# Up-projections of the third and fourth gated network as seven half-block products in place of eight

## What is computed

```python
def conv_ffn(a, w_up, conv_w, w_down):
    g, u = jnp.split(dwconv3(a @ w_up, conv_w), 2, axis=-1)
    return (jax.nn.silu(g) * u) @ w_down

h = h + g2 * conv_ffn(modulate(rms_norm_2(h, norm_ffn[i]), sh2, sc2), ffn_w_up[i], ffn_conv[i], ffn_w_down[i])
```

## Time and profile before

| what | value |
|---|---|
| median of 3 runs | 2995.22 us (2992.68 to 2999.0) |
| the profiled execution | 2993.15 us |
| its span, first to last instruction | 2991.4 us |
| PE busy | 2913.9 us, 97% |
| DVE, ACT, POOL busy | 60%, 43%, 16% |
| PE on the chain that ended last | 93% |

### The profile page before, as it was taken

How to read it: one execution, slowest core, us unless ns; L and a number is a source line. 1 busy time by engine, 2 the same in 40 slices (tenths; PEclk the granted TensorE clock), 3 DMA queues, 4 the chain that set the end, 5 groups by cost and what they waited for, 6 DMA issues and landing times.

```text
span 2991.4 us, 46812 instructions
## 1 busy us (share of the span) xinstructions
PE 2913.9 (97%) x19658; PEld 2583.3 (86%) x19658; DVE 1797.0 (60%) x2666; ACT 1300.3 (43%) x2153; POOL 483.1 (16%) x405
## 2 busy tenths in 40 slices
PE   6998999999999999999999999999999999999999
PEld 6997887899999999999999977667888878788887
DVE  7776664579597453547949757655535543465453
ACT  4575664344243455644424445654323332343231
POOL 0002221123032000002303313001202111121020
PEclk9998997999999999999999999999999999999999
DMA  2210000245554321025545520102232222223232
GB/s 103 89 53 36 2 2 6 75 156 183 170 170 164 113 88 36 1 79 183 176 164 189 188 99 29 43 17 83 94 97 88 97 90 93 91 85 101 90 97 86
DMA packets 79554, 284.34 MB, mean 95 GB/s; under 512 B 8528, under 2 KB 9296, under 8 KB 78576
## 3 DMA queue, kind: packets, MB, share of 16 engines
q1 hardware_dynamic: 79344, 281.35, 28.1%
HBM read 274.96 MB, written 6.36 MB: 94 GB/s over the span
## 4 chain that ended last, share of the span: by engine, by line
PE 93%; DVE 4%; ACT 2%; issue 1%; POOL 1%; DMA 0%; SPq 0%; DVEq 0%; ACTq 0%
PE psum L348 67%; PE psum L2733 2%; PE psum L1893 2%; PE psum L912 2%; PE psum L2104 2%; PE psum L2086 1%; PE psum L2077 1%; PE psum L1269 1%; PE psum L848 1%; PE psum L539 1%; PE psum L1319 1%; PE psum L1286 1%; PE psum L2430 1%; PE psum L2727 1%; PE psum L2721 1%
## 5 line engine op out<-in xcount | busy, mean ns | idle before, releaser
L303 DVE TENSOR_TENSOR wlo<-wraw,whi 128x1024 fp32r<-128x1024 f32 (+2 forms) x398 | 507.7, 1297 | 614.7 <-ACT whi L296 605.8
L296 ACT CAST whi<-wraw 128x1024 fp32r<-128x1024 f32 (+2 forms) x398 | 396.3, 1021 | 495.2 <-PE psum L348 460.6
L431 DVE CUSTOM_DVE_ANT_0 araw<-araw,cond 128x1024 f32<-128x1024 f32 x112 | 181.1, 1654 | 0.0
L348 PE MATMUL psum<-f0xh,whi 128*128 128x264 f32 x704 | 143.1, 285 | 0.0
L348 PE MATMUL psum<-f0xh,wlo 128*128 128x264 f32 x704 | 143.0, 285 | 0.0
L348 PE MATMUL psum<-f0xl,whi 128*128 128x264 f32 x704 | 142.4, 284 | 0.0
L348 PE MATMUL psum<-f1xh,whi 128*128 128x258 f32 x704 | 141.9, 283 | 0.0
L348 PE MATMUL psum<-f1xh,wlo 128*128 128x258 f32 x704 | 141.9, 283 | 0.0
L348 PE MATMUL psum<-f1xl,whi 128*128 128x258 f32 x704 | 141.4, 282 | 0.0
L348 PE MATMUL psum<-f2xh,whi 128*128 128x512 f32 x352 | 139.1, 395 | 1.0 <-DVE f2xl L592 1.0
L348 PE MATMUL psum<-f3xh,whi 128*128 128x512 f32 x352 | 139.1, 395 | 1.0 <-DVE f3xl L592 1.0
(11 more groups left out here) (515 smaller groups left out, 8193.9 us busy)
## 6 DMA issues: line engine op xcount, KB each, us to landing
wraw<-d_w SPq DMA_DIRECT2D x357, 512.0 KB, 3.4
araw<-d_ada SPq DMA_DIRECT2D x112, 512.0 KB, 3.3
wraw<-d_w SPq DMA_DIRECT2D x32, 384.0 KB, 3.6
hn<-d_h SPq DMA_DIRECT2D x4, 528.0 KB, 7.9
hres<-d_h SPq DMA_DIRECT2D x1, 2112.0 KB, 8.2
spill<-hres SPq DMA_DIRECT2D x1, 2112.0 KB, 7.4
hres<-spill SPq DMA_DIRECT2D x1, 2112.0 KB, 8.5
cond<-d_cond SPq DMA_DIRECT2D x2, 1024.0 KB, 4.8
```

The source lines that it names most:

```text
L296: e.copy(whi[0:rows, n % NH, 0:kt * cols], wraw[0:rows, n % NR, 0:kt * cols]).then_inc(*w_hi.up(n))
L303: e.tensor_tensor(wlo[0:rows, n % NH, 0:kt * cols], wraw[0:rows, n % NR, 0:kt * cols], whi[0:rows, n % NH, 0:kt * cols].bitcast(F32), ALU. ...
L348: ins = e.matmul(psum[0:bw, b0 + nb * len(sl) + si, 0:ln], l_ if z == 2 else h_, (xp.lo if z == 1 else xp.hi)[:, k, o:o + ln], start=k == ...
L431: e.tensor_tensor_reduce(out=w, in0=w, in1=self.c[:, col, :], scale=1.0, scalar=0.0, op0=ALU.mult, op1=ALU.add, accum_out=ada[:, ly, blk, ...
```

## The change

In f2 and f3 all pairs but the first two (`PLAIN = 2`) multiply by Strassen's scheme on one level. A pair is a product of a weight matrix of 256 columns by 1024 rows and 512 tokens; each of the three extents is halved, and the eight half-block products become seven of sums and differences of the halves.

- **TensorE**: seven products of 12 matmuls (4 blocks by hi/lo 3) over 256 tokens, 84 in place of 48 of 512 tokens. Products 0 and 1 start in banks b and b + 3. Product 2 adds on top of a copy of bank b in bank b + 1, products 4 and 6 in bank b + 2 on top of a copy of b + 1 (`quad_pe`).
- **ACT**: seven roundings of 128 by 512 in place of two of 128 by 1024; two copies from PSUM to PSUM, two from PSUM into `U` and one from PSUM into `p7`, all of 256 tokens, in place of two copies of 512; the first tap of gate and of value, which DVE had before.
- **DVE**: seven subtractions for `wlo` of 128 by 512 in place of two of 128 by 1024; four taps in place of six; two additions of 256 tokens from PSUM and `p7`.
- **POOL**: four sums of weights per pair, 128 by 512 each (`w_sum_pool`), beside the two operations on the hidden values that it had.
- **Once per network**: sums of the normalized tokens, POOL 16 operations of 128 by 256 and one small one, ACT and DVE twelve each for hi and lo (`turned`).
- `whi` and `wlo` now have six slots of 512 columns: an item is split when the item six half slots before it has been used. SP waits for the last reader of a raw chunk, for its first chunk also for POOL's last sum.

The diff, cut to its core:

```diff
--- before.py
+++ after.py
...
+SEVEN = ("f2", "f3")
+PLAIN = 2
+def by_seven(tag, j):
+    return isinstance(tag, tuple) and tag[0] in SEVEN and tag[1] == "up" and 11 * tag[2] + j >= PLAIN
...
+        for key in ([(n, i) for i in range(7)] if k == 0 else []) if seven else [(n,)]:
+            wide = 1 if seven else 2
+            pos += pos % wide
+            place[key] = pos % halves
+            users = [last[h % halves] for h in range(pos, pos + wide) if h % halves in last]
+            if users:
+                prev[key] = max(users)
+                freed.setdefault(prev[key], []).append(key)
+            for h in range(pos, pos + wide):
+                last[h % halves] = key
+            pos += wide
...
         def w_dma(e, n):
             _, _, _, kt, rows, cols = PLAN[n]
-            if n >= NR:
-                e.wait_ge(*w_lo.at(n - NR))
+            m = n - NR
+            if m >= 0:
+                tag, j, k, *_ = PLAN[m]
+                if not by_seven(tag, j):
+                    e.wait_ge(*w_lo.at(m))
+                elif k == 0:
+                    e.wait_ge(*w_lo.at(m, 4))
+                    e.wait_ge(*w_sum.at(m, 3))
+                else:
+                    e.wait_ge(*w_lo.at(m - 1, 6))
...
+        def factor_of(n, i):
+            return (quarter(n, 0), pair_sum(n), quarter(n, 1), quarter(n + 1, 0), quarter(n, 0), quarter(n + 1, 1),
+                    quarter(n + 1, 0))[i]
...
+        def w_sum_pool(e, n, s):
+            if s == 0:
+                g = SUMS.index((n, 0)) // 4
+                raw_here(e, n)
+                if g >= 2:
+                    e.wait_ge(*w_lo.at(SUMS[4 * g - 8][0], 1))
+                e.tensor_tensor(pair_sum(n), quarter(n, 0), quarter(n, 1), ALU.subtract).then_inc(*w_sum.up(n, 0))
+            elif s == 1:
+                raw_here(e, n + 1)
+                e.wait_ge(*w_sum.at(n, 0))
+                e.tensor_tensor(quarter(n, 1), quarter(n + 1, 1), pair_sum(n), ALU.subtract).then_inc(*w_sum.up(n, 1))
+            elif s == 2:
+                e.wait_ge(*w_sum.at(n, 1))
+                e.wait_ge(*w_lo.at(n, 0))
+                e.tensor_tensor(quarter(n, 0), quarter(n, 1), quarter(n, 0), ALU.add).then_inc(*w_sum.up(n, 2))
+            else:
+                e.wait_ge(*w_lo.at(n, 3))
+                e.tensor_tensor(quarter(n + 1, 0), quarter(n + 1, 0), quarter(n, 1), ALU.subtract).then_inc(*w_sum.up(n, 3))
+        def w_freed(e, split, *key):
+            for item in FREED.get(key, ()):
+                split(e, *item)
...
+            steps = [(b, X(0, first)), (b + 3, T(2)), (b + 1, T(3)), (b, X(4, first)), (b + 2, T(0)), (b + 1, T(1)),
+                     (b + 2, X(4, second))]
+            for i, (bank, operand) in enumerate(steps):
+                e.wait_ge(*w_lo.at(n, i))
+                if i == 0 and bank_free(f, p, 0):
+                    e.wait_ge(*bank_free(f, p, 0))
+                elif i == 1 and bank_free(f, p, 3):
+                    e.wait_ge(*bank_free(f, p, 3))
+                elif i == 2:
+                    e.wait_ge(*f_ev.at(f, p, 0))
+                elif i == 4:
+                    e.wait_ge(*f_ev.at(f, p, 1))
+                elif i == 6:
+                    e.wait_ge(*f_ad.at(f, p, 0))
+                wh, wl = w_place(whi, n, i), w_place(wlo, n, i)
+                for k in range(4):
+                    if p == PLAIN and i == 1:
+                        e.wait_ge(*f_tl.at(f, k, 3))
+                    for z in range(3):
+                        ins = e.matmul(psum[:, bank, 0:half], (wl if z == 2 else wh)[:, k, :], operand(z, k),
+                                       start=i < 2 and k == 0 and z == 0, stop=k == 3 and z == 2, skip_group_check=True)
+                ins.then_inc(*w_used.up(n, i))
...
+            def quad(p, behind):
+                n, b = quad_chunk(f, p), quad_bank(p)
+                if behind:
+                    second_out(p - 1)
+                w_freed(e, w_split_act, *AHEAD[(n, 0)])
+                if behind:
+                    tap(p - 1, 0)
+                e.wait_ge(*w_used.at(n, 0))
+                if bank_free(f, p, 1):
+                    e.wait_ge(*bank_free(f, p, 1))
+                e.activation(psum[:, b + 1, 0:half_], psum[:, b, 0:half_], ACT.Copy).then_inc(*f_ev.up(f, p, 0))
+                w_freed(e, w_split_act, n, 0)
+                e.wait_ge(*w_used.at(n, 1))
+                if p - 2 >= (PLAIN if p < 11 else 11):
+                    e.wait_ge(*f_ad.at(f, p - 2, 1))
+                e.activation(F.p7[:, p % 2, :], psum[:, b + 3, 0:half_], ACT.Copy).then_inc(*f_ev.up(f, p, 7))
+                w_freed(e, w_split_act, n, 1)
+                if behind:
+                    tap(p - 1, 1)
+                e.wait_ge(*w_used.at(n, 2))
+                if bank_free(f, p, 2):
+                    e.wait_ge(*bank_free(f, p, 2))
+                e.activation(psum[:, b + 2, 0:half_], psum[:, b + 1, 0:half_], ACT.Copy).then_inc(*f_ev.up(f, p, 1))
+                w_freed(e, w_split_act, n, 2)
+                e.wait_ge(*w_used.at(n, 3))
+                if p - 2 >= (0 if p < 11 else 11):
+                    e.wait_ge(*f_c.at(f, 2 * (p - 2), 2))
+                e.activation(up_slot(F, 2 * p, 0), psum[:, b, 0:half_], ACT.Copy).then_inc(*f_ev.up(f, p, 2))
+                w_freed(e, w_split_act, n, 3)
+                if behind:
+                    silu(p - 1)
+                w_freed(e, w_split_act, n, 4)
+                w_freed(e, w_split_act, n, 5)
+                if behind:
+                    hidden(p - 1)
...
+            def quad(p, behind):
+                n, b = quad_chunk(f, p), quad_bank(p)
+                w_freed(e, w_split_dve, *AHEAD[(n, 0)])
+                w_freed(e, w_split_dve, n, 0)
+                if behind:
+                    tap(p - 1, 0, 1)
+                w_freed(e, w_split_dve, n, 1)
+                if behind:
+                    tap(p - 1, 0, 2)
+                w_freed(e, w_split_dve, n, 2)
+                if behind:
+                    tap(p - 1, 1, 1)
+                w_freed(e, w_split_dve, n, 3)
+                if behind:
+                    tap(p - 1, 1, 2)
+                e.wait_ge(*f_ev.at(f, p, 7))
+                e.wait_ge(*w_used.at(n, 4))
+                e.tensor_tensor(up_slot(F, 2 * p + 1, 1), psum[:, b + 2, 0:half_], F.p7[:, p % 2, :],
+                                ALU.add).then_inc(*f_ad.up(f, p, 0))
+                w_freed(e, w_split_dve, n, 4)
+                e.wait_ge(*w_used.at(n, 5))
+                e.tensor_tensor(up_slot(F, 2 * p + 1, 0), psum[:, b + 1, 0:half_], F.p7[:, p % 2, :],
+                                ALU.add).then_inc(*f_ad.up(f, p, 1))
+                w_freed(e, w_split_dve, n, 5)
...
+            sums(0)
+            sums(1)
+            weights(PLAIN, (0,))
+            e.wait_ge(*n_lov.at(f, 7))
+            e.memset(F.U[:, :, 0:F.lead], 0.0).then_inc(*zeroed.up(f, 0))
+            e.memset(F.U[:, :, ntok + 1:ntok + 2], 0.0).then_inc(*zeroed.up(f, 1))
+            sums(2)
+            sums(3)
+            weights(PLAIN, (1, 2))
+            hidden(0)
+            weights(PLAIN, (3,))
+            rest(0)
+            for half in range(2):
+                for p in range(11 * half if half else PLAIN, 11 * half + 11):
+                    more_ = p % 11 < 10
+                    if more_:
+                        weights(p + 1, (0, 1, 2))
+                    if p > 11 * half:
+                        hidden(p - 1)
+                    if more_:
+                        weights(p + 1, (3,))
+                    if p > 11 * half:
+                        rest(p - 1)
+                hidden(11 * half + 10)
+                rest(11 * half + 10)
+                if not half:
+                    weights(11, range(4))
...
-            ffn_pe(e, F2, lambda e: e.wait_ge(*res.at("wino", 5)))
+            ffn7_pe(e, F2, lambda e: e.wait_ge(*res.at("wino", 5)))
```

310 lines of the change are left out of this document (269 added, 41 removed).

## The result

The changed kernel takes 3118.77 us (median of four runs, 3116.46 to 3122.09), the kernel before 2996.97 in the same comparison: a ratio of 1.0409 with the interval 1.0391 to 1.0427, 122 us more. The forecast was 3104, 109 more.

The account below looks back on a forecast made before the run. TensorE bounds the kernel before; after the change DVE, taking turns with POOL, bounds the up-projection pairs. Steady pairs 81, edge pairs 1 and starts 27 give +109 us, 3104 us with the median's offset; range 3070 to 3140.

Parts of the forecast that it names:

- TensorE per pair: Up-projection pairs: 84 matmuls of 256 tokens at 0.117 us take 9.8 us, saving 1.4 us a pair.
- DVE by itself: DVE's 13 operations in a pair: 8.6 us, less 1.1 for overlap of queued instructions, 7.5 us.
- POOL's price of 1.07: Each of POOL's six operations in a pair costs DVE 1.07 us, since the two take turns reading SBUF.
- The period: Steady pairs 3 to 9 and 13 to 20: 13.9 us against 11.2 before, +2.7 each, 81 us on 30.
- DVE itself never waits: Steady pairs: ACT rounds DVE's pieces of weights well ahead and product 4 is long done, so DVE's sum sets the period.
- the signs that would prove it wrong: Profile: POOL at 1.3 us on DVE at 0.68; PE waiting on ACT or DMA; up-projection clock 0.50; DVE with gaps.
- Edge pairs: Last pair of each half and first two of the second half: 11.1 to 12.0 us, +1 us in all.
- The start: Each network, norm to end of pair 2: 50 us against 36, +13.5 each, 27 in all, ends 15 and 35.
- The upper bound of the forecast: Whole kernel: 3135 us, from 14.4 us a pair and the start's upper end of 35.
- The engines side by side: Rival: DVE and POOL run beside each other, TensorE bounds at 10.1 us a pair, -36 us, 2959 us; chance 0.07.
- The half: Rival: only DVE's and POOL's exclusive times remain, 12.95 us or less a pair, 3062 to 3075 us; chance 0.05.
- The clock as the bound: Rival: TensorE at half clock, matmuls 0.234 us, 19.7 us a pair, about +300 us, 3300 us; chance 0.04, from 3140 up.

Follow-up runs that it names:

- The narrow sums: Changed kernel with POOL's four sums of weights per pair cut to 16 columns of one block: 2975.28 us, ratio 0.9924.
- the kernel with VectorE's sums and the early addition: Changed kernel with the four sums of weights moved from POOL to DVE and product 6's addition ahead of the last tap and fourth split: 3035.11 us, ratio 1.0124.
- the run with everything on VectorE: The kernel with VectorE's sums and the early addition, with the hidden product and its rest also moved from POOL to DVE: 3092.87 us, ratio 1.0311.
- the kernels with nothing to read for GpSimd: Changed kernel with POOL's four sums of weights per pair made memsets of 512 columns, 2968.12 us; or cut to 16 columns, 2975.28 us.
- the kernel with halved sums: Changed kernel with POOL's four sums of weights per pair computing 256 of 512 columns: 3028.65 us, ratio 1.0098.

## Why the prediction was right, point by point

**TensorE per pair** (84 x 0.117 = 9.8, and 10.1 with the wait): right. The narrow sums give pairs of 10.10, and pairs without any wait take 9.89 (pair 12 in the kernel with VectorE's sums and the early addition).

**DVE by itself, 7.5 us, and POOL's price of 1.07.** Right within what can be read: 7.5 + 6 x 1.07 = 13.9 against 13.94 with the clock at 1.00. What was measured is the sum; the two terms were not measured apart. Thirteen overlaps of 0.1 are 1.3 and not the 1.1 that the forecast gave back, which would make DVE's own time 7.3 and a POOL operation 1.11. Taken apart by the forecast's 7.5, a sum of 512 columns costs 1.08, one of 256 0.51, a sum done by DVE itself 0.58 to 0.72.

**The period.** Forecast 13.9, measured 14.08. The step that failed is "DVE itself never waits". It waits 0.47 and 0.42 us in a pair for ACT's roundings, which wait for places that TensorE frees with product 6 and the next pair's first product, and those are late by the spells at half the clock. The forecast had the clock only as a rival of 3300 us and had put a granted clock of 0.50 in the up-projections, and DVE with gaps, among the signs that would prove it wrong. Both came: the spells about once in a pair, at a cost of 0.14 us, +4 us on 30 pairs, and 4.7 us of gaps in 98. TensorE's wait before product 6, by the distance of starts, is 2.4 to 2.6 us in four of pairs 3 to 9, 3.9 in two and 1.5 in one, for the 4 forecast, since product 6 and the next pair's first product take up to 4.6 us in place of 2.8.

**"The period is DVE's sum"** held in size, and was too simple in kind: moving the addition, which changes no length, took 0.24 us at the same clock (0.38 in all), and the run with everything on VectorE showed a loop over two engines' lists that takes 13.6 us with DVE at 84%. That the forecast's time came out this near is in part luck of this list, in which DVE's gaps are small.

**Edge pairs.** Forecast +1 us in all; pairs 10, 11, 12 and 21 take 12.1, 11.1, 12.0 and 11.5, +1.9 us in each network, 4 in both. In pairs 10 and 21 TensorE still waits 1.1 us before product 6.

**The start.** Forecast: pair 2 ends 50 us after the norm began, +13.5. Measured: from 2056.70 to 2107.63, 50.9 us, against 2052.09 to 2054.66 and three pairs, 36.2: +14.8 in f2, and +14.6 in f3. The first pair takes 15.84, about 16 forecast. (The forecast's own 50 less 36 is 14, not 13.5.)

**The sum.** 30 x 2.88 = 86, starts 30, edges 4: 120, against 109 forecast. The profiled executions differ by 123.3; 4.6 of them lie ahead of the norm of f2, where the kernels don't differ, so the three terms are about 1 us too much. The terms were each 3 to 5 us too small, all in the same direction. The upper bound of the forecast was added wrongly: 14.4 us a pair and a start term of 35 give 96 + 1 + 35 = 132, some 3127 us, and not 3135. The result lies inside that too.

**The rivals.** The engines side by side (2959) is out; its pairs of 10.1 are what the kernels with nothing to read for GpSimd show. The half (12.95 a pair) is out for this kernel. The clock as the bound is out: with it at 1.00 the pairs are 0.14 us shorter. Its price was also too high, since at 0.50 the matmuls of 256 columns come 0.213 us apart (starts at 2119.64 and 2120.92 with six steps between) and not 0.234.

## What to carry to other kernels

An operation that GpSimd does for an already busy VectorE is not free: where VectorE has two inputs in SBUF and GpSimd reads SBUF, each waits for the whole of the other, and VectorE lost 1.08 us to a GpSimd sum that it does itself in 0.6 to 0.7. Price a change by the engine that is second in line, with its neighbours' turns in the sum, before trusting what the first engine saves. And a sum of lengths is a bound on one engine only: where three engines hand over in lists of fixed order, follow one hand-over round the loop (a product at the end of one list, a rounding that blocks the next) before taking a gap for room.

## What the runs showed of the hardware that was not expected

Short spells of the lower clock come in steady work too. TensorE idle for 2.3 us in a pair of 14 was followed by 2.7 us at 0.50, about once in a pair, in stretches where the granted clock is 0.88 in the mean; one wait of the same length was not followed by any. In the kernel with halved sums, which waits 1.7 us in a pair of 11.7, the clock stays at 1.00 (its row above), and so it does with matmuls put into the wait.

A GpSimd memset of 512 columns takes 0.53 us and leaves VectorE's two-input operations at 0.69 us, the length that they have alone. A GpSimd sum of 16 columns takes 0.22 to 0.68 us in the mean, by the line it stands in, and the VectorE subtraction shown beside it still takes 0.69.
